# A split value projection, a new order in heads and gates, and a last expert pair by column quarters

## The chip, the cores and the metric

The kernel runs on one core of a Trainium2 chip. Its time is the device time of one execution in microseconds (us). The engines are named as the profile names them: PE is TensorE (PEld its weight loads), DVE is VectorE, ACT is ScalarE, POOL is GpSimd, SP issues most transfers.

## The reference

One layer over 320 tokens (256 prompt frames and 64 sample frames), model width 1024, all in float32:

```python
h   = layer_norm(x)
q, f_pre, i_v, g_o, u_a, u_b, gate_a, gate_b = split(h @ w_in)
logf = log_sigmoid(f_pre) + log1p(lb * exp(-f_pre));  k = (1 - lb) * sigmoid(-f_pre)
# per head (8 heads, 128x128 state): S_t = diag(f_t) S_{t-1} + k_t v_t^T,  o_t = S_t^T q_t
o   = rms_norm(o) * silu(g_o);                 y_a = o @ w_o_a
u   = u_a * sigmoid(u_b);  c = causal depthwise conv, 31 taps;  y_b = silu(layer_norm(c)) @ w_o_b
x   = layer_norm(ALPHA * h + (sigmoid(gate_a) * y_a + sigmoid(gate_b) * y_b) @ w_out)
# router: best of 4 groups, then 2 of its 4 experts
y   = sum_e gates[e] * ((silu(x @ w_gate[e]) * (x @ w_up[e])) @ w_down[e])
out = layer_norm(ALPHA * x + y)
```

## The kernel before

All five engines run programs written out by hand; semaphores alone tie them together, and each engine goes through its program in order. A helper `signal` issues an instruction and then waits for its own end, and a `Chain` does the same.

**Heads.** `head_turn(cur, nxt, prev, pprev)` is one turn of a software pipeline over the eight heads, written once for each engine. In turn n, PE projects the forget logits of head n (`cur_f`) and its queries (`cur_q`); both are split projections (`project`): each float32 operand is a high half in the fp32r format (`wh`, `xh`, written by ACT's `w_high`) and a low half, what is left (`wl`, written by DVE's `w_low`), and PE runs three products for each of 8 row blocks, 24 matmuls of 320 columns. The value projection (`cur_v`, `value_tile`) is not split: 24 matmuls of full float32, tile by tile, whose result has tokens on its rows. For head n-1 PE runs the transposes `prev_kT`, the within-block attention at seven levels of halving (`levels`), `prev_states` and `prev_out`; for head n-2 the sum of squares (`rms`). ACT runs the logarithms and exponentials of the forget gates (`forget`), the copies out of PSUM, `w_high`, and one exponential over all levels (`level_exp`, 2176 columns), then `tile_exp`, `prev_square` and the stores of the states. DVE runs `forget_in` with the scan, `level_decay` (7 instructions), the masks over the level products (`level_mask`, `last_mask`), `w_low`, `prev_final`, `query_side` (7) and `carry_side`. POOL runs `key_decay` (7), seven sums over the levels (`level_sums`, `last_sums`) on which `prev_out` waits, and `key_side` (7).

**Convolution and gates.** PE then runs eight split projections for the convolution (`conv_value`, `conv_gate`) and 24 for the gates (`gates`), with ACT's `u_high`, `t_high` and DVE's `u_low`, `t_low` as their halves. Between these DVE runs the 124 taps of the convolution (`conv_taps`), of which 101 stand ahead of the end of the last `t_low`. PE runs `recurrent(0)` and `(1)` and then sums the columns for the mean, which waits for all taps (`conv_done`).

**Mixing and router.** PE multiplies by `w_out` tile by tile. After the third tile it transposes the new x (`to_features`) and computes the router logits; DVE selects the experts, PE counts positions, and `keep_busy` matmuls, whose result nobody reads, fill PE's time. DVE's `picks` makes the 0/1 matrices by which PE gathers 64 slots for each of two experts.

**Experts.** The 16 experts are taken in 8 pairs. Each pair has 12 groups of weights (4 gate, 4 up, 4 down) of 2 MB each; the ring has 8 slots, and SP reloads a slot when `group_used` says that PE is done with it. `sums_back` puts the sums into PSUM ahead of the last pair's `down`, `last_scatter` adds the last pair's output there, and the closing layer norm (`stats2`, `norm_apply`) reads PSUM and is followed by the store of the result.

Of the kernel before, what the change touches and what calls it, by code (L numbers as in the profile page):

```python
# [21 lines left out]
ALU = mybir.AluOpType  # L22
# [43 lines left out]
def shape_constants():  # L66
# [9 lines left out]
    c[:, COFF["i64"]:COFF["i64"] + CAP] = np.arange(CAP)  # L76
# [10 lines left out]
LOGIT_BANKS = [6, 7, 4]  # L87
# [32 lines left out]
def build(nc, a, o):  # L120
    with ExitStack() as ctx:
# [13 lines left out]
        wring = ring[:, :, :, :, :].rearrange("p g b k n -> p (g b k n)").rearrange("p (g m k n) -> p g m k n", g=SLOTS, m=2, k=2)  # L135
        wslot = ring[:, :, :, :, :].rearrange("p g b k n -> p (g b k n)").rearrange("p (g n) -> p g n", g=SLOTS)
# [50 lines left out]
        (hq, hk, hV, he, hw, hls, hb, heb, hqeb, hkde, hkT, hAM, hAS, hSA, hosq, hrs, hebl, _, hSst, hSo) = carve(  # L187
            0, 2 * T, 2 * T, 384, T, T, T, T, T, T, T, 384, 3 * LW, 384, P, T, T, 4, 892, 2 * P, 2 * P)
# [22 lines left out]
            0, D, 3 * D, KT * NE, NE, *[48] * 8, 72, 24, 24, 144, 18, 20, 4, KT * P, D, D, KT * P, D, 384, 384, 384)  # L211
# [10 lines left out]
        cur = cur.rearrange("p (w t e) -> p w t e", w=3, t=3)  # L222
# [20 lines left out]
                 "osq_ready rms_done rstd_ready rstd_exp o_out so_ready so_stored hc_dve hp_dve hc_act hp_act hc_pool hp_pool v_sb round")  # L243
# [14 lines left out]
                 "eos_ready y_done y_added pick_step gpick_step y_back")  # L258
# [52 lines left out]
        def _(sp):  # L311
# [101 lines left out]
            with sp.Fori(1, PAIRS // 2) as i:  # L413
                for g in range(2 * PARTS):
                    sp.wait_ge(e["group_used"], 2 * PARTS * i + g - SLOTS + 1)
                    load_group(i, g)
            sp.wait_ge(routed, 1)
            more = sp.value_load(flag[0:1, :], min_val=0, max_val=1)
            with sp.If(more != 0):
                with sp.Fori(1, ROUNDS) as r:  # L420
                    with sp.Fori(0, PAIRS // 2) as i:
                        for g in range(2 * PARTS):
                            sp.wait_ge(e["group_used"], PARTS * PAIRS * r + 2 * PARTS * i + g - SLOTS + 1)
                            load_group(i, g)
# [10 lines left out]
        def _(pe):  # L435
# [46 lines left out]
            def cur_f(i, b, first):  # L482
                pe.wait_ge(wlo_ready, 2 * (2 * i + b) + 1)
# [4 lines left out]
            def cur_q(i, b, first, after_rms):  # L488
                pe.wait_ge(wlo_ready, 2 * (2 * i + b) + 2)
# [6 lines left out]
            def value_tile(b, t):  # L496
                t0, n = TILES[t]
                for k in range(KT):
                    last = mm(ps[0:n, 3, t * P:t * P + P], xT[:, k, t0:t0 + n], sh[:, b, 3, k, :], k == 0, k == KT - 1)
                return last  # L500

            def cur_v(i, b, first):
                pe.wait_ge(wh_in[b], i * 48 + (16, 48)[b])
                if not first:
                    pe.wait_ge(h["v_sb"], 2 * i + b)
# [43 lines left out]
            def prev_out(i, b, first):  # L549
# [7 lines left out]
                pe.wait_ge(h["as_ready"], 2 * n1 + 1)  # L557
# [5 lines left out]
                pe.wait_ge(h["as_ready"], 2 * n1 + 2)  # L563
# [9 lines left out]
            def head_turn(cur, prev, pprev, first=False, first_prev=False):  # L573
# [5 lines left out]
                if first or first_prev:  # L579
                    cur_q(*cur, first, False)  # L580
                if pprev:
# [28 lines left out]
            rms(3, 0)  # L610
            prev_kT(3, 1, False)
            levels(3, 1, False)
            prev_states(3, 1)
# [1206 lines left out]
```

## Time and profile before

| what | value |
|---|---|
| time, median of 3 runs | 912.35 us (911.97 to 913.24) |
| the profiled execution | 911.96 us, its span 910.1 us |
| PE busy | 848.2 us, 93% of the span |
| DVE busy | 397.4 us, 44% |
| ACT busy | 227.5 us, 25% |
| POOL busy | 108.1 us, 12% |
| bytes read from HBM | 245.89 MB |

Busy time is what the engine's instructions took; a matmul's end is modelled. Roughly, the heads last from 37 to 178 us, convolution and gates to 314 us, mixing to 412 us, the router to 441 us and the experts to 896 us.

### The profile page before, as it was taken

The numbers are of one execution on the slowest core, as the hardware profiler recorded it, in microseconds if no ns is written. First come the engines' busy times: TensorE is split into PE (matmuls) and PEld (weight loads), VectorE is DVE, ScalarE is ACT, GpSimd is POOL, SyncE is SP. The second block draws the span as 40 slices with busy tenths as digits, with TensorE's granted clock in tenths as the row PEclk, the third lists the DMA queues.
The fourth block names the chain that finished last, engine by engine and source line by source line (L and its number), as shares of the span: only waits on it lengthen the run. The fifth ranks groups of instructions, "written<-read, shape, count | busy, mean of one in ns | idle before, by whom it ended". The sixth has DMA issues, their size and how long they took to land.

```text
span 910.1 us, 12810 instructions
## 1 busy us (share of the span) xinstructions
PE 848.2 (93%) x4904; PEld 532.4 (58%) x4904; DVE 397.4 (44%) x720; ACT 227.5 (25%) x358; POOL 108.1 (12%) x173
## 2 busy tenths in 40 slices
PE   4999999999999999999999999999999899898983
PEld 3989888898989866546554353535435244252330
DVE  6787788879999823215310313103031040310205
ACT  6566666653356131003010011000100001000001
POOL 1366667620000000000000000000000000000000
PEclk9999999999999999998999999999999999999997
DMA  8222222524436523905499999999999999999951
GB/s 302 71 79 80 78 78 85 188 80 154 171 104 237 212 107 153 372 0 208 163 429 428 428 428 428 426 428 427 429 427 429 428 428 428 428 428 428 427 255 59
DMA packets 30420, 248.95 MB, mean 274 GB/s; under 512 B 4462, under 2 KB 7918, under 8 KB 17962
## 3 DMA queue, kind: packets, MB, share of 16 engines
q1 hardware_dynamic: 27840, 247.07, 66.2%
q10 hardware_dynamic: 2538, 1.32, 0.5%
q8 instruction: 27, 0.44, 0.2%
q14 instruction: 15, 0.12, 0.0%
HBM read 245.89 MB, written 2.48 MB: 273 GB/s over the span
## 4 chain that ended last, share of the span: by engine, by line
PE 53%; DVE 19%; DMA 15%; POOL 5%; issue 4%; ACT 3%; POOLq 0%; DVEq 0%; ACTq 0%; SPq 0%
PE ps L437 52%; DMA ring<-in_w_up_e 8%; DMA ring<-in_w_gate_e 7%; DVE ar L1503 6%; DVE split_t L1511 3%; POOL ring L1240 2%; DVE ring L1390 1%; DVE ring L1403 1%; POOL ring L1226 1%; PE ps L772 1%; DVE split_w L1349 1%; POOL ar L1255 0%; DVE mid L1521 0%; POOL ar L1253 0%; DVE split_w L1354 0%
## 5 line engine op out<-in xcount | busy, mean ns | idle before, releaser
L437 PE MATMUL ps<-ring,ar 128*64 128x512 f32 (+1 forms) x1120 | 268.2, 594 | 10.6 <-DMA ring<-in_w_gate_e 3.9
L437 PEld LDWEIGHTS ps<-ring,ar 128*64 128x64 f32 (+1 forms) x1120 | 99.1, 140 | 168.5 <-issue 152.6
L437 PE MATMUL ps<-ring,xT 128*64 128x512 f32 (+2 forms) x896 | 161.4, 458 | 7.0 <-DMA ring<-in_w_gate_e 6.7
L437 PEld LDWEIGHTS ps<-ring,xT 128*64 128x64 f32 (+1 forms) x896 | 84.3, 152 | 79.0 <-issue 63.8
L1720 DVE TENSOR_TENSOR ar<-ar,ps 128x512 f32<-128x512 f32 (+1 forms) x42 | 28.7, 684 | 224.4 <-PE ps L437 224.4
L437 PE MATMUL ps<-split_x,split_t 128*128 128x320 f32 x672 | 101.7, 313 | 4.7 <-DVE split_t L1511 4.1
L437 PEld LDWEIGHTS ps<-split_x,split_t 128*128 128x128 f32 x672 | 100.1, 191 | 6.0 <-issue 3.8
L437 PE MATMUL ps<-split_x,split_w 128*128 128x320 f32 x480 | 80.4, 324 | 6.6 <-DVE split_w L1354 2.7
L437 PEld LDWEIGHTS ps<-split_x,split_w 128*128 128x128 f32 x480 | 73.8, 195 | 11.1 <-issue 2.5
L437 PE MATMUL ps<-ar 128*64 128x64 f32 (+6 forms) x304 | 74.1, 375 | 3.1 <-ACT ar L1174 1.2
L1503 DVE SCALAR_TENSOR_TENSOR ar<-ar,params 128x350 f32<-128x350 f32 x116 | 67.7, 584 | 4.1
L437 PEld LDWEIGHTS ps<-ar 128*128 128x128 f32 (+2 forms) x304 | 35.6, 170 | 39.0 <-DVE ar L1720 19.5
L1708 DVE TENSOR_TENSOR ar<-ar,ps 128x1024 f32<-128x1024 f32 x8 | 9.8, 1222 | 87.5 <-PE ps L437 87.5
L437 PEld LDWEIGHTS ps<-ar,mid 128*128 128x128 f32 x384 | 43.5, 192 | 6.7 <-issue 5.7
L437 PE MATMUL ps<-ar,mid 128*128 128x128 f32 x384 | 45.0, 277 | 0.2 <-DVE ar L1682 0.2
L1240 POOL TENSOR_TENSOR ring<-ring,ar 128x160 f32<-128x160 f32 (+1 forms) x56 | 40.2, 718 | 6.6 <-issue 2.3
L1174 ACT ACTIVATE ar<-ps 128x1024 f32<-128x1024 f32 x8 | 8.2, 1024 | 116.3 <-PE ps L437 116.3
L1164 ACT ACTIVATE ar<-ps 128x1024 f32<-128x1024 f32 x8 | 8.2, 1025 | 111.3 <-PE ps L437 111.3
L1297 DVE BATCH_NORM_STATS2 stats<-ps 128x6 f32<-128x512 f32 (+1 forms) x12 | 8.4, 696 | 61.1 <-PE ps L437 60.8
L437 PE MATMUL ps<-mid,ring 128*128 128x320 f32 x128 | 34.9, 432 | 0.0
L916 ACT ACTIVATE split_t<-ring 128x1024 fp32r<-128x1024 f32 x24 | 25.5, 1061 | 27.3 <-PE ps L437 26.8
L1226 POOL TENSOR_TENSOR ring<-ar 128x160 f32<-128x160 f32 (+1 forms) x56 | 25.7, 459 | 51.8 <-DVE ar L1381 48.0
(190 smaller groups left out, 721.8 us busy)
## 6 DMA issues: line engine op xcount, KB each, us to landing
ring<-in_w_gate_e SPq DMA_DIRECT2D x32, 2048.0 KB, 27.5
ring<-in_w_up_e SPq DMA_DIRECT2D x32, 2048.0 KB, 25.9
ring<-in_w_down_e SPq DMA_DIRECT2D x32, 2048.0 KB, 31.7
ring<-in_w_in SPq DMA_DIRECT2D x56, 512.0 KB, 4.3
ring<-in_w_o_a SPq DMA_DIRECT2D x8, 512.0 KB, 5.9
ring<-in_w_out SPq DMA_DIRECT2D x1, 4096.0 KB, 14.6
ring<-in_w_o_b SPq DMA_DIRECT2D x4, 512.0 KB, 5.1
ar<-in_x_prompt SPq DMA_DIRECT2D x2, 512.0 KB, 4.5
```

The source lines that it names most:

```text
L437: return pe.matmul(out, lhsT, rhs, start=start, stop=stop)
L772: last = pe.transpose(ps[:, k // 4, (k % 4) * P:(k % 4) * P + P], eh[:, k * P:k * P + P], ident)
L916: signal(act, act.activation(t_hi[1 - b][q][1], stl[:, b, 8 * q:8 * q + 8].rearrange("p k n -> p (k n)"), ACT.Copy), thi_ready, 2 * n + q + 1)
L1226: ins = pool.tensor_tensor(xv, bv[:, :, hs - 1:hs].to_broadcast([P, w // (2 * hs), hs]), bv[:, :, 0:hs], ALU.subtract)
L1240: ins = pool.tensor_tensor(xv, xv, kv, ALU.mult)
L1349: signal(dve, dve.tensor_tensor(piece(wl, q), sh[:, b, q].rearrange("p k n -> p (k n)"), piece(whF, q), ALU.subtract), wlo_ready, 2 * n + ...
L1390: ins = dve.tensor_tensor(xv[:, :, hs:2 * hs], bv[:, :, hs:2 * hs], bv[:, :, hs - 1:hs].to_broadcast([P, w // (2 * hs), hs]), ALU.subtract)
L1403: ins = dve.tensor_tensor(xv, xv, qv, ALU.mult)
L1503: vc(dve.scalar_tensor_tensor(acc, uc[:, c, j:j + CW], vt[:, c, j:j + 1], acc, ALU.mult, ALU.add))
L1511: signal(dve, dve.tensor_tensor(t_lo[1 - b][q][1], stl[:, b, 8 * q:8 * q + 8].rearrange("p k n -> p (k n)"), t_hi[1 - b][q][0], ALU.subtract),
L1708: signal(dve, dve.tensor_tensor(eh, ehs, ps[:, 2:4, :].rearrange("p b n -> p (b n)"), ALU.mult), e["eh_ready"], n + 1)
L1720: signal(dve, dve.tensor_tensor(yv, yv, ps[0:c, 4 + j % 2, :], ALU.add), e["y_added"], 6 * n + j + 1)
```

## The change

The value projection becomes a third split projection. Its result has features on its rows, so ACT copies it (`v_features`) and PE transposes it back (`v_tokens`) before the old copy `v_copy`; both copies of V now stand around `level_exp`, `v_features` ahead of it. Each head has one more `w_high` and one more `w_low`. On PE, `levels` goes ahead of `prev_kT`. On DVE, both masks and a new `level_fold` go ahead of `level_decay`; the fold takes over the first of POOL's sums, and POOL's seven sums become three. The copy `hebl` moves from DVE to ACT. `u_high`, `u_low`, `t_high`, `t_low` go by single halves, and fewer taps stand ahead of each `t_low` (98 ahead of the end of the last one). The first tile's transposes go between the second and third tile of the mixing, the second group of logits goes ahead of the third tile's transposes, and the filler matmuls go from 2+8+2 to 6+1. `picks` makes its matrices in one instruction instead of six, as does `gate_picks`; PE starts the gate groups on the first half of the gathered slots. The last pair's `w_down` is stored by column quarters (`w_down_end`, the same bytes) and `down`, copy, scatter and sum go quarter by quarter; `sums_back` is gone.

```diff
 def cur_v(i, b, first):
+    pe.wait_ge(wlo_ready, 3 * n + 3)
+    project(3, piece(wh, 2), piece(wl, 2)).then_inc(h["v_done"], 1)
-    value_tile(b, 0)
-    value_tile(b, 1)
-    value_tile(b, 2).then_inc(h["v_done"], 1)
+def v_tokens(i, b):
+    pe.wait_ge(h["vT_sb"], 2 * i + b + 1)
+    for t, (t0, n) in enumerate(TILES):
+        last = pe.transpose(ps[0:n, 3, t * P:t * P + P], hvT[:, t0:t0 + n], ident)
...
 # PE, head_turn
     if pprev:
         rms(*pprev)
-    if prev:
-        prev_kT(*prev, first_prev)
-        levels(*prev, first_prev)
+        levels(*prev, False)
+        prev_kT(*prev, False)
+        cur_q(*cur, False, True)
         prev_states(*prev)
-    if pprev:
-        cur_q(*cur, False, True)
     cur_v(*cur, first)
     if prev:
         prev_out(*prev, first_prev)
+    v_tokens(*cur)
...
 # PE, router
-keep_busy(2)
 logits(0)
+logits(1)
 to_features(x1, x1_ready, x1T_done, x1T_sb, X1_BANKS, 2, 3)
-logits(1)
 logits(2)
-keep_busy(8)
+keep_busy(6)
...
 # DVE, head_turn
     forget_in(*cur, first or first_prev)
-    level_decay(*cur)
     if prev:
         level_mask(*prev, first_prev)
         last_mask(*prev, first_prev)
+        level_fold(*prev)
+    level_decay(*cur)
...
+def level_fold(i, b):
+    signal(dve, dve.tensor_tensor(hAM[:, :, 0:3 * BLK], hAM[:, :, 0:3 * BLK], hAM[:, :, 4 * BLK:LW], ALU.add), h["fold_ready"], n + 1)
...
 # DVE, picks
-for t in range(3):
-    for m in range(2):
-        ins = dve.tensor_scalar(ePm[:, t, 64 * m:64 * m + 64], i64, cur[:, 0, t, m:m + 1], cur[:, 1, t, m:m + 1], ALU.is_equal, ALU.mult)
+signal(dve, dve.tensor_tensor(pm4, slots_wide, slot_of(cur[:, 0]), ALU.is_equal), e["pick_ready"], n + 1)
...
+def last_down(i, b, c):
+    for k in range(KT):
+        for m in range(2):
+            last = mm(ps[64 * m:64 * m + 64, 6 + c % 2, 0:QN], ehT[:, k, 64 * m:64 * m + 64], w[:, m, k, :], k == 0, k == KT - 1)
...
 # PE, last pair
+last_down(i, b, 0)
+last_down(i, b, 1)
-sums_back()
+last_scatter(0)
+last_down(i, b, 2)
+last_scatter(1)
+last_down(i, b, 3)
+last_scatter(2)
+last_scatter(3)
```

ACT in a turn of the heads, from before the exponential over the levels to the stores of the states. Before, the copy of the queries (L958) and of the crossing blocks (L1005) stand behind the exponential L978, and the copies of V are L970 and L971:

```order
L978 ACTIVATE ring<-ring 128x2176
L958 ACTIVATE ar<-ps 128x320
L1005 ACTIVATE ar<-ps 64x2x64
L986 ACTIVATE ar<-ar 128x320
L988 ACTIVATE ar<-ar 128x128 x2
L988 ACTIVATE ar<-ar 128x64
L895 ACTIVATE split_w<-ring 128x1024
L970 ACTIVATE ar<-ps 128x256
L971 ACTIVATE ar<-ps 64x128
L1021 ACTIVATE ar<-ps 128x320
L1027 DMA out_new_hgrn_prompt<-ar 128x128
```

And now, where the exponential is L1006, `v_features` is L991, the copies of V are L998 and L999, the copy `hebl` is L1015 and the high halves are L919:

```order
L991 ACTIVATE ar<-ps 128x320
L1006 ACTIVATE ring<-ring 128x2176
L998 ACTIVATE ar<-ps 128x256
L999 ACTIVATE ar<-ps 64x128
L1014 ACTIVATE ar<-ar 128x320
L1015 ACTIVATE ar<-ar 128x2
L1017 ACTIVATE ar<-ar 128x128 x2
L1017 ACTIVATE ar<-ar 128x64
L919 ACTIVATE split_w<-ring 128x1024 x2
L1050 ACTIVATE ar<-ps 128x320
L1056 DMA out_new_hgrn_prompt<-ar 128x128
```

The copies of the queries and crossing blocks went ahead of the exponential, a copy of V stands right ahead of it, and between it and the stores stand one more high half and the small copy.

DVE at the start of a turn, from the scan (the last instruction of `forget_in`) on. Before, the seven instructions of `level_decay` are L1390 and the masks L1426 and L1433:

```order
L1381 SCALAR_TENSOR_TENSOR ar<-cst,ar 128x320
L1390 TENSOR_TENSOR ring<-ar 128x2x64
L1390 TENSOR_TENSOR ring<-ar 128x5x32
L1390 TENSOR_TENSOR ring<-ar 128x10x16
L1390 TENSOR_TENSOR ring<-ar 128x20x8
L1390 TENSOR_TENSOR ring<-ar 128x40x4
L1390 TENSOR_TENSOR ring<-ar 128x80x2
L1390 TENSOR_TENSOR ring<-ar 128x160
L1426 TENSOR_TENSOR ar<-ps,mid 128x896
L1433 TENSOR_TENSOR ar<-ps,mid 64x448
```

Now the masks are L1464 and L1471, the fold is L1475 and `level_decay` is L1429:

```order
L1420 SCALAR_TENSOR_TENSOR ar<-cst,ar 128x320
L1464 TENSOR_TENSOR ar<-ps,mid 128x896
L1471 TENSOR_TENSOR ar<-ps,mid 64x448
L1475 TENSOR_TENSOR ar<-ar 128x3x192
L1429 TENSOR_TENSOR ring<-ar 128x2x64
L1429 TENSOR_TENSOR ring<-ar 128x5x32
L1429 TENSOR_TENSOR ring<-ar 128x10x16
```

Masks and fold now stand between the scan and the differences that the exponential over the levels waits for.

PE in the last pair, from the transposes of the gate matrices on. Before, `sums_back` (from `cst`, the identity) stands ahead of `down` (from `ring`):

```order
L776 MATMUL ps<-cst,ar 128x64
L437 MATMUL ps<-ar,cst 128x512 x4
L437 MATMUL ps<-ar,cst 64x512 x2
L437 MATMUL ps<-ring,ar 64x512 x32
L437 MATMUL ps<-ar 128x512 x4
L437 MATMUL ps<-ar 64x512 x2
```

Now two quarters of `down` come first, and scatters of 256 columns stand between the quarters:

```order
L792 MATMUL ps<-cst,ar 128x64
L448 MATMUL ps<-ring,ar 64x256 x32
L448 MATMUL ps<-ar 128x256 x2
L448 MATMUL ps<-ar 64x256
L448 MATMUL ps<-ring,ar 64x256 x16
L448 MATMUL ps<-ar 128x256 x2
L448 MATMUL ps<-ar 64x256
L448 MATMUL ps<-ring,ar 64x256 x16
```

The identity matmuls are gone, and only the scatters of the last two quarters are left behind the last `down`.

## Rows read from the trace of the kernel before

**Rows 1.** Windows: length, busy PE, PEld, DVE, ACT, POOL, PE clock, DMA, GB/s
```profile
460.00:480.00 20.00, 19.52 (x119) 11.51 (x117) 2.60 (x3) 1.63 (x3) 0.00 (x0) 1.00 1.00 428
```

**Rows 2.** Timeline of PE in a turn: start, us, engine, instructions
```profile
85.58 3.78 PE L437 MATMUL ps<-split_x,split_w 128*128 128x320 f32 x24
...
89.20 5.62 PE L437 MATMUL ps<-ring,xT 128*128 128x128 f32 x48
```

**Rows 3.** Timeline of DVE: first instruction of a turn, turns 2 and 7
```profile
62.93 0.49 DVE L1373 SCALAR_TENSOR_TENSOR ar<-ps,ar 128x320 f32<-128x320 f32 x1 [2.55 <-ACT ar L950]
...
163.53 0.49 DVE L1373 SCALAR_TENSOR_TENSOR ar<-ps,ar 128x320 f32<-128x320 f32 x1 [2.26 <-ACT ar L950]
```

**Rows 4.** Timeline of DVE in the heads
```profile
37.87 4.33 DVE L1403 TENSOR_TENSOR ring<-ring,ar 128x128 f32<-128x128 f32 x7
...
85.75 3.39 DVE L1390 TENSOR_TENSOR ring<-ar 128x128 f32<-128x128 f32 x7
...
89.35 1.09 DVE L1426 TENSOR_TENSOR ar<-ps,mid 128x896 f32<-128x896 f32 x1 [0.21 <-DVE ring L1390]
...
90.63 0.62 DVE L1433 TENSOR_TENSOR ar<-ps,mid 64x448 f32<-64x448 f32 x1 [0.19 <-DVE ar L1426]
...
94.40 3.57 DVE L1403 TENSOR_TENSOR ring<-ring,ar 128x128 f32<-128x128 f32 x7
...
98.10 1.38 DVE L1349 TENSOR_TENSOR split_w<-ring,split_w 128x1024 fp32r<-128x1024 f32 x1
```

**Rows 5.** Timeline of ACT in a turn (ACTq: issue of a transfer)
```profile
89.60 2.02 ACT L978 ACTIVATE ring<-ring 128x2176 f32<-128x2176 f32 x1 [2.26 <-POOL ring L1226]
...
96.66 0.38 ACT L970 ACTIVATE ar<-ps 128x256 f32<-128x256 f32 x1 [1.16 <-PE ps L437]
...
98.40 0.39 ACTq L1027 DMA_DIRECT2D out_new_hgrn_sample<-ar  x1
...
100.58 0.44 ACT L944 ACTIVATE ar<-ps 128x320 f32<-128x320 f32 x1 [2.77 <-PE ps L437]
```

**Rows 6.** Timeline of PE in the gates
```profile
224.16 35.46 PE L437 MATMUL ps<-split_x,split_t 128*128 128x320 f32 x240 [1.66 <-DVE split_t L1511]
...
261.79 37.06 PE L437 MATMUL ps<-split_x,split_t 128*128 128x320 f32 x240 [2.17 <-DVE split_t L1511]
```

**Rows 7.** A window of PE: length, busy, PE clock, DMA, GB/s
```profile
263.00:264.00 1.00, 1.00 (x5) 0.50 0.00 0
```

**Rows 8.** Timeline where taps end and the mean begins
```profile
313.95 0.58 DVE L1505 SCALAR_TENSOR_TENSOR mid<-ar,params 128x350 f32<-128x350 f32 x1
...
314.91 2.52 PE L437 MATMUL ps<-mid,ones 128*128 128x350 f32 x8
```

**Rows 9.** Timeline of the router, from the last logits to the first gate group
```profile
418.06 4.11 PE L437 MATMUL ps<-ar,xT 128*128 128x16 f32 x32
...
429.87 0.07 DVE L1656 MEMSET ar<- 64x16 f32 x1
...
431.16 0.32 PE L437 MATMUL ps<-ar,cst 128*128 128x48 f32 x2
...
432.46 2.07 DVE L1682 TENSOR_SCALAR ar<-cst,ar 128x64 f32<-128x64 f32 x6
...
434.58 5.62 PE L437 MATMUL ps<-ar,mid 128*128 128x128 f32 x48 [0.20 <-DVE ar L1682]
...
441.10 11.38 PE L437 MATMUL ps<-ring,ar 128*64 128x512 f32 x52 [0.90 <-ACT ar L1160]
```

**Rows 10.** Timeline of the last pair and the closing norm
```profile
869.34 5.53 PE L437 MATMUL ps<-ar,cst 128*128 128x512 f32 x12 [1.03 <-ACT ar L1170]
...
874.80 13.95 PE L437 MATMUL ps<-ring,ar 128*64 128x512 f32 x64
...
889.94 5.57 PE L437 MATMUL ps<-ar 128*128 128x512 f32 x12 [1.18 <-ACT ar L1174]
...
898.82 1.28 DVE L1301 SCALAR_TENSOR_TENSOR ar<-ps,mv,mid 128x1024 f32<-128x1024 f32 x1 [1.55 <-issue]
```

More of the change, by code:

```diff
@@ L416, in _ @@
                     load_group(i, g)
+            end_i = PAIRS // 2 - 1
+            for g in range(2 * PARTS):
+                sp.wait_ge(e["group_used"], 2 * PARTS * end_i + g - SLOTS + 1)
+                if g < 2 * PARTS - 4:
+                    load_group(end_i, g)
+                else:
+                    sp.dma_start(wslot[:, g % SLOTS, :], column(a["w_down_end"], g % 4)).then_inc(group_in[g % SLOTS], 16)
             sp.wait_ge(routed, 1)
@@ L784, in down, with scatter @@
                     both(6, ehT, g).then_inc(e["group_used"], 1)
-            def scatter(n):
-                pe.wait_ge(e["eos_ready"], n + 1)
+            def scatter(n, late=0):
+                pe.wait_ge(e["eos_ready"], n + 1 + 3 * late)
                 pe.wait_ge(e["eGT_sb"], n + 1)
@@ L846, in late_pair @@
                 down(n, i, b)
-                scatter(n)
+                scatter(n, 1)
             more = pe.value_load(flag[0:1, :], min_val=0, max_val=1)
@@ new lines, in gates @@
+                signal(act, act.activation((mT, sgb)[q][:, bass.ds(n - 4, 1), :].rearrange("p o n -> p (o n)"), ps[:, GATE_BANKS[2 * b + q], 0:T], ACT.Sigmoid), sgt_ready, 2 * n + q + 1)
+            for i in range(2):
+                for b in range(2):
+                    for q in range(2):
+                        t_high(i + 1, b, q)
+                        out_gates(i, b, q)
+            with act.Fori(2, NG // 2 - 1) as i:
+                for b in range(2):
+                    for q in range(2):
+                        t_high(i + 1, b, q)
+                        gates(i, b, q)
@@ L1129, in _ @@
+            for b in range(2):
+                for q in range(2):
+                    gates(NG // 2 - 1, b, q)
             act.preload_act_table_set("natural_log_exp_and_others")
@@ L1181, in expert_pair @@
                 hidden_copy(n)
-                down_copy(n)
+                if end:
+                    for c in range(4):
+                        last_copy(c)
+                else:
+                    down_copy(n)
             def late_pair(i, b):
@@ L1196, in _ @@
             expert_pair(PAIRS // 2 - 1, 1, end=True)
+            act.preload_act_table_set("natural_log_exp_and_others")
+            for t in range(3):
+                rstd_of(var2, rstd2, step, t)
             more = act.value_load(flag[0:1, :], min_val=0, max_val=1)
             with act.If(more != 0):
+                act.preload_act_table_set("silu_and_others")
                 with act.Fori(1, ROUNDS) as r:
@@ L1462, in head_turn @@
                     w_low(*nxt, 0)
+                else:
+                    u_low(0, 0)
                 if prev:
@@ L1467, in head_turn @@
                 query_side(*cur)
+                carry_side(*cur, first)
                 if nxt is None:
-                    u_low(0)
+                    u_low(0, 1)
                 elif not first:
                     w_low(*nxt, 1)
-                carry_side(*cur, first)
+                if nxt:
+                    w_low(*nxt, 2)
             head_turn((0, 0), (0, 1), None, None, first=True)
@@ L1482, in _ @@
             last_mask(3, 1, False)
+            level_fold(3, 1)
             pprev_out(3, 0)
-            u_low(1)
+            u_low(1, 0)
+            u_low(1, 1)
             vc = Chain(dve, conv_step)
```

435 lines of the change are left out of this document (221 added, 214 removed).

## The prediction

> **What bounds the kernel now.** I read the page first (PE busy 93%, every other engine under half), then the chain of waits, then windows of 20 us, and last the timeline of each stage, since the change touches all of them but the middle of the experts.
>
> The experts are bound by the transfers, although PE looks full: in [rows 1] the DMA engines are busy all of the time at 428 GB/s, and each group of weights is awaited. The stream begins when the first slot comes free and its bytes are fixed. So the expert stage moves as a block with its start, and what shortens PE's work inside it (halves of the gathered slots, fewer matrix instructions) is worth nothing there. Only its start and what lies behind the last transfers can give time.
>
> In the heads a turn lasts 20.12 us (five turns between the two starts of [rows 3]). PE is nearly full in it, but it isn't alone: VectorE starts each turn after waiting 2 us or so for ScalarE's logarithms [rows 3]. VectorE's own work in a turn is thus about 18.1 us. From the convolution on, PE and VectorE are level: the last tap ends 0.4 us before the mean that needs it [rows 8], and PE waits 1.66 and 2.17 us for low halves [rows 6].
>
> **Heads.** A value projection takes 5.62 us now and a split one 3.78 us [rows 2]; with some 0.6 us of transposes back, PE saves 1.2 us a turn. I don't count it, because two other loops become longer.
>
> ScalarE with VectorE: from the end of the exponential over the levels, 91.62, to the end of the second store's issue, 98.79, is 7.17 us [rows 5]. Of it 1.16 us were a wait for V and 1.04 us the two copies that go ahead; a second high half adds 1.09 (those are 128x1024 like the first), the small copy 0.23 and the wait to begin 0.17: 6.46 us. `forget` takes 2.8 us (100.58 to VectorE's start of the turn at 103.4). VectorE's `forget_in` and scan take 2.7 us (83.05 to 85.75 in the turn of [rows 4]). Then come the masks, 1.09 + 0.19 + 0.62 us [rows 4], and the fold of 576 columns, by the 1.38 us of 1024 columns [rows 4] about 0.8; with their gaps 2.9 us. `level_decay` takes 3.4 us and the exponential 2.02, with gaps 5.6. The loop is 6.46 + 2.8 + 2.7 + 2.9 + 5.6 = 20.46 us. Before, the masks ran under the exponential and cost this loop nothing.
>
> VectorE alone: 18.1 + 0.8 (fold) + 0.1 + 1.5 (a third low half) - 0.4 (copy gone) = 20.1 us if its queries take 3.57 us, and 20.9 us if they take the 4.33 us of the turn in which POOL's keys ran beside all of them [rows 4]. I take 20.45 us a turn, +0.33, five times: +1.6 us. The first two turns: VectorE goes from its queries to the next turn in one piece, so the third low half less the copy costs 1.2 us; in the second turn the masks come into the loop, +0.9. So the last turn begins 3.7 us later, at 167.2 instead of 163.53.
>
> The two prices of the queries differ by what POOL did beside them: 3.57 us where its keys ran beside only the second half, 4.33 us where they ran beside all of them [rows 4]. In the new order queries and keys both begin when the exponential ends, or nearly. The Trainium skill, "GPSIMD Engine Reference" (Key points), says that GpSimd shares its SBUF interfaces with VectorE and that instructions of VectorE with two SBUF inputs contend with it; by that rule the sum below would be 3.2 us larger (rival B), by the shorter row as it stands. The trace agrees in these two rows.
>
> **Convolution and gates.** In the last turn PE waits some 3 us for `prev_square`, which now stands behind three high halves; a wait of 2.17 us made the PE clock fall to half for about 3 us [rows 6, 7], so I put 1.0 us on the levels behind it. Against that, `u_low(2)` no longer stands behind eight taps, 0.5 us. Fewer taps ahead of each `t_low` take away PE's waits of 1.66 and 2.17 us, but VectorE has the same 124 taps and halves to do and is without a pause, so `conv_done` is where VectorE puts it; PE, 4 us early, then waits in front of the mean in one piece, is ready a little sooner (-0.2), and restarts at half clock: by the two equal stretches of 240 matmuls in [rows 6], 37.06 - 35.46 = 1.6 us. From there to the router PE is the bound, so all of this counts: 1.0 - 0.5 - 0.2 + 1.6 = +1.9 us.
>
> **Router.** The last logits end 1.1 us earlier: two groups of logits, 4.1 us with the third [rows 9], no longer stand behind the third tile's transposes, but one tile's transposes (1.0 us) came ahead of the third tile's mix. The selection ended at 429.94 and PE came to it at 431.16, late by its own filler [rows 9]; with six fillers it comes on time: 428.9. PE's counts and one filler then take 2.3 us, VectorE's picks 0.6 instead of 2.07 (384 columns at the rate of the fold), so the gather begins at 431.2 instead of 434.58. The first gate group began 0.9 us after the gather's end, after a copy [rows 9]; it now starts on the first half at once: 436.9 instead of 441.1. -4.2 us.
>
> **Last pair.** 869.34 to 874.87 are `sums_back` [rows 10], which goes. The four quarters of `down` cost as many columns, 13.95 us, and two scatters of a quarter (5.57 / 4 = 1.4 us each) lie between them: 869.3 + 13.95 + 2.8 = 886.1. Two more scatters: 888.9, where PE's last matmul ended at 895.5 before. PE took its four groups without a wait, the last from 885.3 on [rows 10]; the last quarter now begins at 882.6, and if its weights landed only at 885.3, 2.7 us of this would be lost. VectorE then has for each tile an add of 256 columns (0.45), statistics of 512 (0.7) and a short one (0.3) behind the last scatters: to 892.5. The branch, 1.55 us [rows 10], now stands behind the norm. Six instructions of 1.3 us end at 900.4 instead of 906.7. -6.3 us; the copies of a quarter, 0.3 to 0.4 us on ScalarE, lie beside matmuls, and if they didn't it would be 1 us more.
>
> **Sum.** 3.7 + 1.9 - 4.2 - 6.3 = -4.9 us. The profiled execution took 911.96 us, so 907.0; the median of the runs is 0.4 above it: **907.4 us**, 0.5% faster. 0.2% (1.8 us) is about what a measurement of this kernel can tell from no change.
>
> **Rivals.**
>
> A. PE was the bound of the heads and the reordered loops fit around it: a turn becomes 20.12 - 1.2 = 18.9 us. For it: the page's 93%. Against: VectorE's 20.1 us. Seven turns give -8.4 instead of +3.7, so 895.3; halfway, with a turn of 19.5 us, five of them give -3.1 and the sum 902.7. Chance 0.2 together.
>
> B. VectorE and POOL disturb each other fully: the turn is 20.9 us, and the masks wait now and then. +0.45 for six turns, and 0.5 for the second turn: 910.6. Chance 0.15.
>
> C. The PE clock falls in every turn. PE now waits between the next forget projection and `rms`, because ScalarE's square comes late: its projection ends some 14.7 us into the turn and the square 16.6, 1.9 us. The trace has 1.66 us without and 2.17 us with a fall [rows 6, 7]. If it falls, levels, queries and V lie in the slow stretch, each turn loses 1.6 us less 0.15 us of slack, six times 8.7 us, and 0.7 in the second: 916.8, slower. It decides from 1.3 us a turn. Chance 0.07. In a sentence of its own: the Trainium skill, "TensorE: Matmul & The Clock Gate" (HAM oscillation), warns of exactly this, a clock that falls again at each repeated idle stretch.
>
> D. The router's filler is now too short and the gather runs at half clock. Half speed for 3 us of the gather gives 2.8 back at most: 910.2. Chance 0.08.
>
> E. The last pair's narrower matmuls don't run in pairs at full rate: 256 columns behind each weight load instead of 512. A fifth more on 13.95 us is 2.8 us: 910.2. Chance 0.05.
>
> The forecast itself: 0.45, within 904 to 909.5.
>
> **Numbers.** The range is 898 to 912: below it lies half of A, above it C and the ends of B and D. Faster by over 0.2% means below 910.5: forecast, A, and parts of B, D and E: 0.78. Within: 0.13. Slower: 0.09.
>
> **What would show it.** Turn starts of VectorE 20.3 to 20.6 us apart, and the last at about 167; at 163 or below, A. No long wait of VectorE for ScalarE's logarithms ahead of a turn. PE's idle time per turn in one or two pieces near 2 us with the clock at 1.00 (C: 0.5 in windows). A wait of PE ahead of the mean, which begins near 318.9, and none over 1 us in the gates. The first gate group at about 442.5. PE's last scatter 6.6 us nearer to the last landing than before, the norm's end 6.3. The prediction is wrong if a turn is off by half a microsecond (3 us in all), or if the transfers have slack that I don't see, so that the start of the stream doesn't set their end.

## The result, and the profile after

The changed kernel takes **921.88 us** (median, 921.66 to 925.07) beside 912.80 us for the kernel before on the same chip: ratio 1.0108, 95% interval 1.0085 to 1.0132. It is slower by 1%, where 907.4 us were forecast and 898 to 912 us allowed. The profiled execution has a span of 919.6 us where before had 910.1: +9.5 us.

I split these 9.5 us at the places at which the prediction split its sum. First the heads: VectorE's first instruction of turns 2 and 7 (start, us, instruction, in brackets the wait and its releaser), to be held against [rows 3].

```profile
66.58 0.49 DVE L1412 SCALAR_TENSOR_TENSOR ar<-ps,ar 128x320 f32<-128x320 f32 x1 [1.55 <-ACT ar L973]
...
179.95 0.49 DVE L1412 SCALAR_TENSOR_TENSOR ar<-ps,ar 128x320 f32<-128x320 f32 x1 [1.97 <-ACT ar L973]
```

The last turn starts at 179.95 instead of 163.53: **+16.4 us** (forecast +3.7). Five turns take 22.67 us each, not 20.12. Then the mean, on PE's timeline, for [rows 8]:

```profile
317.18 8.78 PE L448 MATMUL ps<-mid,ring 128*128 128x320 f32 x32
332.13 5.04 PE L448 MATMUL ps<-mid,ones 128*128 128x350 f32 x8 [6.18 <-DVE mid L1554]
```

It starts 17.2 us later than before (314.91), 0.8 us more than the heads explain, after a wait of 6.18 us for the last tap, and takes 5.04 us instead of 2.52 since the clock has fallen: **+3.3 us** (forecast +1.9). The first gate group, the first quarters of `down` and the last instruction of the norm answer to [rows 9, 10]:

```profile
451.32 5.62 PE L448 MATMUL ps<-ar,mid 128*128 128x128 f32 x48
456.88 13.52 PE L448 MATMUL ps<-ring,ar 128*64 128x512 f32 x62
...
884.40 7.13 PE L448 MATMUL ps<-ring,ar 128*64 128x256 f32 x64 [0.48 <-ACT ar L1203]
...
914.93 1.28 DVE L1341 SCALAR_TENSOR_TENSOR ring<-ring,rstd,ar 64x1024 f32<-64x1024 f32 x1
```

The gate group starts 15.8 us later than at 441.10, so the router gave 16.4 + 3.3 - 15.8 = **4.0 us** (forecast 4.2). The norm ended at 906.69 and now ends at 916.21, +9.5, so the last pair gave 15.8 - 9.5 = **6.3 us** (forecast 6.3). Three of the four terms are right within 1.4 us; the heads are off by 12.7.

Where the heads lose them is seen in the turn that starts at 90.19. ScalarE from the copy `v_features` (L991) on:

```profile
99.30 0.44 ACT L991 ACTIVATE ar<-ps 128x320 f32<-128x320 f32 x1 [3.45 <-PE ps L448]
99.90 2.02 ACT L1006 ACTIVATE ring<-ring 128x2176 f32<-128x2176 f32 x1 [0.17 <-DVE ring L1429]
103.58 0.38 ACT L998 ACTIVATE ar<-ps 128x256 f32<-128x256 f32 x1 [1.66 <-PE ps L517]
```

The exponential ends at 101.92, but on ScalarE all that stands behind it, up to the next turn's `forget`, waits for `v_copy` (L998), and `v_copy` waits 1.66 us for the transposes `v_tokens` (L517). PE at that time, and VectorE from the masks on:

```profile
100.97 1.69 PE L448 MATMUL ps<-ar 128*128 128x128 f32 x10 [1.77 <-DVE mid L1493]
102.59 0.90 PE L517 MATMUL ps<-cst,ar 128*128 128x128 f32 x3
```

```profile
92.90 1.09 DVE L1464 TENSOR_TENSOR ar<-ps,mid 128x896 f32<-128x896 f32 x1 [0.21 <-DVE ar L1420]
94.18 0.62 DVE L1471 TENSOR_TENSOR ar<-ps,mid 64x448 f32<-64x448 f32 x1 [0.19 <-DVE ar L1464]
94.83 0.76 DVE L1475 TENSOR_TENSOR ar<-ar 128x576 f32<-128x576 f32 x1
95.63 4.19 DVE L1429 TENSOR_TENSOR ring<-ar 128x128 f32<-128x128 f32 x7
99.98 0.55 DVE L1493 SCALAR_TENSOR_TENSOR mid<-ps,params,ar 128x320 f32 x1 [0.16 <-DVE ring L1429]
```

The transposes stand behind `prev_out`, and `prev_out` waits 1.77 us for `pprev_out` (L1493), which frees its bank and stands behind masks, fold and `level_decay` on VectorE. In the kernel before it stood behind `level_decay` and the masks too, and nobody waited for it:

```profile
109.50 5.62 PE L437 MATMUL ps<-ring,xT 128*128 128x128 f32 x48
111.83 0.55 DVE L1451 SCALAR_TENSOR_TENSOR mid<-ps,params,ar 128x320 f32 x1 [0.17 <-DVE ar L1433]
115.06 1.10 PE L437 MATMUL ps<-ar 128*128 128x128 f32 x8
```

In this turn, which starts at 103.40, it ended 9.0 us into the turn, and PE came to `prev_out` only at 11.7, after its long value projection. In the changed kernel it ends 10.3 us into the turn, because of the fold and the slower `level_decay`, and PE, with the shorter projection, is there already at 9.0. So PE's wait is new, but `prev_out` itself comes no later in the turn than before; what is new is that ScalarE's copy stands behind it and ahead of `tile_exp`. And `level_decay` (L1429) takes 4.19 us instead of 3.39 [rows 4]. Over the heads, the waits by engine, line and releaser (total, times, longest) are:

```profile
PE ps L448 <- ACT ar L1050: 11.6, 7, 3.1
PE ps L448 <- DVE mid L1493: 10.3, 6, 2.0
...
ACT ar L991 <- PE ps L448: 24.0, 7, 3.5
ACT ar L998 <- PE ps L517: 8.0, 6, 2.2
```

L1050 is `prev_square`, for which `rms` waits. The largest number, 24.0 us ahead of `v_features`, is not the one that counts: in five of the turns the exponential behind it still waits for `level_decay`, above for 0.17 us.

**Theory.** The heads lose 8 us to `v_copy` ahead of `tile_exp`, which hands every lateness of PE to the next turn, and 4 us to the slower `level_decay` (0.7 us a turn by the rows, over six turns). **Rivals:** the falls of PE's clock; PE's loop through `prev_square`; the masks ahead of `level_decay` by themselves; the split itself.

### The profile page after: what moved, and what is told of

It is laid out like the page before. It is cut to its first block, busy times and chain, and to the rows that moved or that the text cites. A ratio compares the mean times of both kernels' runs of the same rounds, so it can differ in the third digit from the quotient of the medians.

```text
span 919.6 us, 12462 instructions
## 1 busy us (share of the span) xinstructions
PE 837.2 (91%) x4790; PEld 529.4 (58%) x4790; DVE 399.1 (43%) x661; ACT 241.8 (26%) x385; POOL 80.2 (9%) x141
## 3 DMA queue, kind: packets, MB, share of 16 engines
q10 hardware_dynamic: 2538, 1.32, 0.5%
## 4 chain that ended last, share of the span: by engine, by line
PE 52%; DVE 21%; DMA 16%; ACT 8%; issue 2%; ACTq 1%; DVEq 0%; SPq 0%
PE ps L448 50%; DMA ring<-in_w_gate_e 11%; DVE ar L1552 7%; DMA ring<-in_w_up_e 4%; DVE ring L1429 3%; DVE split_t L1559 3%; ACT split_w L919 2%; ACT ar L1017 1%; DVE ar L1464 1%; DVE ar L1475 1%; DVE ar L1420 1%; DMA ar<-in_x_prompt 1%; ACTq L1056 1%; PE ps L788 1%; ACT ar L973 1%
## 5 line engine op out<-in xcount | busy, mean ns | idle before, releaser
L448 PE MATMUL ps<-ring,ar 128*64 128x512 f32 (+2 forms) x1184 | 269.6, 571 | 10.4 <-DMA ring<-in_w_gate_e 3.9
L448 PEld LDWEIGHTS ps<-ring,ar 128*64 128x64 f32 (+1 forms) x1184 | 103.7, 140 | 163.2 <-issue 146.1
L448 PE MATMUL ps<-split_x,split_w 128*128 128x320 f32 x672 | 115.9, 331 | 8.4 <-ACT ar L1062 3.3
L448 PE MATMUL ps<-ring,xT 128*64 128x512 f32 x512 | 116.2, 594 | 6.9 <-DMA ring<-in_w_gate_e 6.9
L448 PEld LDWEIGHTS ps<-split_x,split_w 128*128 128x128 f32 x672 | 107.7, 203 | 14.0 <-ACT ar L1062 2.9
L448 PEld LDWEIGHTS ps<-ring,xT 128*64 128x64 f32 x512 | 41.6, 136 | 77.1 <-issue 67.8
L448 PE MATMUL ps<-ar 128*64 128x64 f32 (+8 forms) x316 | 75.3, 370 | 10.8 <-DVE mid L1493 10.3
L1272 POOL TENSOR_TENSOR ring<-ar 128x160 f32<-128x160 f32 (+1 forms) x56 | 28.3, 505 | 80.4 <-DVE ar L1420 76.6
L1286 POOL TENSOR_TENSOR ring<-ring,ar 128x160 f32<-128x160 f32 (+1 forms) x56 | 30.4, 544 | 26.0 <-ACT ring L1006 16.5
L1429 DVE TENSOR_TENSOR ring<-ar 128x160 f32<-128x160 f32 (+1 forms) x56 | 30.5, 544 | 1.9
```

The source lines that it names most:

```text
L448: return pe.matmul(out, lhsT, rhs, start=start, stop=stop)
L1272: ins = pool.tensor_tensor(xv, bv[:, :, hs - 1:hs].to_broadcast([P, w // (2 * hs), hs]), bv[:, :, 0:hs], ALU.subtract)
L1286: ins = pool.tensor_tensor(xv, xv, kv, ALU.mult)
L1429: ins = dve.tensor_tensor(xv[:, :, hs:2 * hs], bv[:, :, hs:2 * hs], bv[:, :, hs - 1:hs].to_broadcast([P, w // (2 * hs), hs]), ALU.subtract)
```

## The experiments

All times are medians, with the ratio to the kernel before and its 95% interval; "turn" is the mean of the five turns 2 to 7. The first three, `copy_late` and `filled` are made on the changed kernel, `copy_sync` and `copy_decay` on copy_late.

### out_first: `pprev_out` ahead of the masks

```diff
 # DVE, head_turn
+    pprev_out(*pprev)
     level_mask(*prev, first_prev)
     last_mask(*prev, first_prev)
     level_fold(*prev)
     level_decay(*cur)
-    pprev_out(*pprev)
```

> Edit: on VectorE the output of the head before the last (pprev_out, 0.55 us) goes ahead of masks, fold and decay. The theory: a turn of the heads is 22.7 us instead of 20.1 because ScalarE's v_copy, which stands ahead of all that follows the exponential, waits 1.0 to 2.2 us (8.0 us in 6) for v_tokens, and these stand on PE behind prev_out, which waits for pprev_out (10.3 us in 6). Two loops run through this wait: one by VectorE (masks, fold, decay, exponential, copies, forget) and one by PE (rms, levels, queries, V, v_features, exponential, copies, high halves, prev_square, rms). If the PE loop sets the turn, the whole wait is given back: 6 turns by 1.3 us, about 914 us. If the VectorE loop does, pprev_out itself (0.59 us) now lies in it: about 918 us. The rivals (VectorE slowed by POOL, or PE's slow clock) expect no change, 921 to 923 us.

918.32 us (1.0056, 1.0039 to 1.0073), turn 21.71 us. `v_copy` waits no more, and the time is that of the second case: the loop by VectorE, with `pprev_out` in it, sets the turn. PE's waits for `prev_square` grew from 11.6 to 18.9 us while the turn became shorter.

### square_first: `prev_square` ahead of two high halves

```diff
 # ACT, head_turn
     tile_exp(*cur, first)
+    prev_square(*prev, first_prev)
     w_high(*nxt, 1)
     w_high(*nxt, 2)
-    prev_square(*prev, first_prev)
     store_states(*prev)
```

> Edit: on ScalarE prev_square goes ahead of the two high halves (2.2 us), the stores stay behind them. The PE loop (PE waits 11.6 us in 7 for prev_square before rms) becomes 2.2 us shorter, the VectorE loop stays as it is. If the PE loop alone sets the turn, about 911 us; if the VectorE loop is as long, no change (within 1 us of 922) and PE's wait only moves from rms to another place.

918.31 us (1.0051, 1.0035 to 1.0067), turn 22.48 us. Between the two cases: PE's waits for `prev_square` fell from 11.6 to 1.0 us, but 13.5 us in 6 for `rstd` came ahead of the queries, and ScalarE's copy of the queries, ahead of the exponential, waits 8.8 us instead of 2.6. The waits for `v_copy` fell to 1.9 us in 2, and yet the turn is only 0.2 us shorter: the wait mostly moved.

### decay_first: `level_decay` ahead of the masks

```diff
 # DVE, head_turn
+    level_decay(*cur)
     level_mask(*prev, first_prev)
     last_mask(*prev, first_prev)
     level_fold(*prev)
-    level_decay(*cur)
```

> Edit: on VectorE level_decay goes back ahead of masks and fold, as before the change. The VectorE loop becomes 2.6 us shorter, the PE loop stays. If the VectorE loop alone sets the turn, about 909 us; if the PE loop does or both are level, no change to speak of (within 2 us of 922): the exponential then waits for v_features, which wait for PE's V projection (24.0 us in 7).

935.32 us (1.0250, 1.0233 to 1.0268), turn 24.28 us. I expected no case of this kind. The waits say why:

```profile
PE ps L448 <- POOL ar L1300: 21.4, 7, 3.4
...
ACT ar L998 <- PE ps L517: 20.1, 6, 4.1
```

With the masks late POOL's sums (L1300) are late, `prev_out` waits for them, and `v_copy` for the transposes behind it, 20.1 us instead of 8.0. It is the theory's mechanism, made worse, and the turn became 1.6 us longer. And the loop by VectorE did not become 2.6 us shorter, as I had expected. ScalarE in the turn that starts at 118.58:

```profile
126.07 0.27 ACT L1034 ACTIVATE ar<-ps 64x128 f32<-64x128 f32 x1 [3.53 <-DVE ar L1464]
...
128.24 2.02 ACT L1006 ACTIVATE ring<-ring 128x2176 f32<-128x2176 f32 x1
```

L1034 is the copy of the crossing blocks. It waits for the mask L1464, and the change put it ahead of the exponential. So the exponential begins 9.7 us into the turn here and 9.7 us in the changed kernel (99.90 in the turn from 90.19), whichever of masks and `level_decay` comes first; in the kernel before, with this copy behind it, it began at 6.6 us (89.60 from 83.05). This run therefore doesn't say what the masks in VectorE's loop cost.

### tail_router: heads, convolution and gates as before

The edit takes back all parts of the change up to the gates; those of the router and the last pair stay.

> Edit: heads, convolution and gates as before; only the router part (first tile's transposes, logits, fillers, picks, gate groups on the first half) and the last pair by column quarters are new. By the stages of the two traces router and last pair together gave 10 to 11 us: 902 us. If the gain of either hangs on the late start of the stream, or the transfers have slack, it would be less: 905 to 908 us.

**902.37 us** (0.9885, 0.9868 to 0.9901). The two late parts give 10.4 us, with 10.5 forecast. The rest of the change costs 19.5 us.

### copy_late: `v_copy` in its old place

```diff
 # ACT, head_turn
-    v_copy(*cur, first)
     tile_exp(*cur, first)
     w_high(*nxt, 1)
     w_high(*nxt, 2)
+    v_copy(*cur, first)
     prev_square(*prev, first_prev)
```

> Edit: the changed kernel with ScalarE's v_copy back behind tile_exp and the high halves, its place before the change; all else of the change stays. The theory (v_copy ahead of tile_exp hands PE's lateness on to forget): the wait of 8.0 us in 6 goes as with out_first, and pprev_out does not enter the VectorE loop, so a turn of 21.1 us: about 915 us. If v_copy's place costs nothing by itself (the masks ahead of decay are all of it): 918 to 922 us.

**913.61 us** (1.0010, 1.0000 to 1.0020), turn 21.15 us. One line moved gives 8.3 us, and PE waits as long for `pprev_out` as in the changed kernel; only ScalarE's `tile_exp` and high halves no longer stand behind that wait. VectorE, turns 2 and 7, and the waits:

```profile
65.92 0.49 DVE L1412 SCALAR_TENSOR_TENSOR ar<-ps,ar 128x320 f32<-128x320 f32 x1 [1.61 <-ACT ar L973]
...
171.66 0.49 DVE L1412 SCALAR_TENSOR_TENSOR ar<-ps,ar 128x320 f32<-128x320 f32 x1 [0.99 <-ACT ar L973]
```

```profile
PE ps L448 <- DVE mid L1493: 10.2, 6, 2.0
PE ps L448 <- ACT ar L1050: 7.0, 4, 2.4
```

### split_old: the split value projection in the old order

On tail_router. PE, ScalarE and VectorE keep the order of before; `v_features` stands behind `tile_exp`, `v_copy` where it was, the fold behind the masks.

> Edit: tail_router (heads in the order of before) with the split value projection: third high and low half, v_features behind tile_exp, v_copy in its old place, v_tokens, the fold on VectorE behind the masks and POOL's three sums. The theory (the orders cost, not the split): PE is the bound of the heads before and has 1.2 us less to do, but prev_out now waits for POOL's sums; 899 to 903 us. If the split itself is what costs (halves on ScalarE and VectorE, contention): over 906 us.

920.43 us (1.0092, 1.0073 to 1.0111), turn 21.92 us: far off, 18 us slower than tail_router. PE has less to do and waits 18.4 us in 7 for POOL's sums ahead of `prev_out`, with the transposes and the next forget projection behind it. The last turn starts 16.4 us later than in tail_router. Of this 9.0 us lie in the five turns, and 5.0 us are there when the second head's turn starts (48.77 instead of 43.76), by this edit's own place for `v_features`: in the first turn it stands behind `tile_exp`, PE waits 6.42 us for it, and the two projections behind that wait take 9.75 us instead of tail_router's 7.31, at a granted clock of 0.50 to 0.72 from 38 to 46 us. So the new order is not the only culprit: in this form of the old one the split gains nothing either, since what PE saves is spent in front of the sums. The change's order with `v_copy` late (copy_late) is the better home for it.

### gates_new, gates_rec, tail_rec: the wait in front of the mean

gates_new is tail_router with the new gates (`t_high`, `t_low` by halves, new places of the taps). gates_rec adds this, and tail_rec is this on tail_router without the new gates:

```diff
 # PE, after the gates
     recurrent(1)
+    recurrent(2)
     pe.wait_ge(conv_done, 4)
...
     last.then_inc(cmean_done, 1)
-    recurrent(2)
     recurrent(3)
+    recurrent(4)
```

> Edit: tail_router with the gates by single halves (t_high, t_low) and the new places of the taps; heads and the halves for the convolution as before. The theory: PE loses its waits of 1.66 and 2.17 us in the gates and gets one in front of the mean, in one piece, and restarts at half clock. In the changed kernel the mean began 0.8 us later against the heads, and 2.5 us went at half clock: 905.5 us, 3 us slower than tail_router. If the order of the taps costs nothing: 902.4 us.

904.11 us (0.9905, 0.9888 to 0.9921): 1.7 us slower than tail_router, not 3. Its mean began 0.8 us earlier than tail_router's and took 4.94 us instead of 2.52.

> Edit: gates_new with PE's recurrent(2) ahead of the mean, so that 4.4 us of its wait are filled with work, and recurrent(4) ahead of the variance in its place. If the wait ahead of the mean and the slow clock behind it are the price of the new gates, both go (4.4 + 2.5 us): 899 to 900 us. If VectorE's taps set the time whatever PE does meanwhile, 905 us as gates_new.

**897.70 us** (0.9835, 0.9819 to 0.9851), the fastest of all. In PE's timeline the wait is 1.88 us and the mean runs at full clock:

```profile
301.35 13.08 PE L448 MATMUL ps<-mid,ring 128*128 128x320 f32 x48
316.32 2.62 PE L448 MATMUL ps<-mid,ones 128*128 128x350 f32 x8 [1.88 <-DVE mid L1542]
```

> Edit: tail_router (gates as before) with recurrent(2) ahead of the mean. There PE is not early, the mean follows recurrent(1) without a wait. If PE's own work sets the time there, the order is worth nothing: 902.4 us. Then the new gates alone cost 1.7 us, recurrent(2) alone gives nothing, and both together gave 4.7 us (gates_rec).

902.92 us (0.9898, 0.9881 to 0.9914), as tail_router. So the new gates alone cost 1.7 us, `recurrent(2)` alone gives nothing, and the two together give 4.7: the gates gather PE's waits into one, and only then is there something to fill. The 1.7 us are small (the intervals of the two ratios overlap); that they are real I take from the trace, where 0.8 us earlier and 2.4 us slower give 1.6.

### copy_sync: both decays begin together

```diff
 # POOL, head_turn, on copy_late
+    pool.wait_ge(h["fold_ready"], 2 * cur[0] + cur[1])
     key_decay(*cur)
```

> Edit: copy_late, with POOL's key_decay waiting for VectorE's fold, so that both decays begin together, as in the kernel before. There VectorE's level_decay took 3.39 us beside POOL's 3.70; in the changed kernel it starts 2.8 us behind POOL's and takes 3.98 to 4.20. If that offset costs the 0.8 us, level_decay is back at 3.4 us; POOL ends some 0.3 us behind it, so 0.4 us a turn is won: about 911 us. The sums come 2.5 us later, though, and prev_out, v_tokens and the next forget projection stand behind them: by that loop a turn of 20.8 us at least, and if it is longer than that the time stays at 913 to 915 us. If the 0.8 us have another cause, level_decay stays at 4.0 to 4.2 us.

927.81 us (1.0169, 1.0151 to 1.0188), turn 23.42 us. The two questions have two answers. `level_decay` is back at its old time:

```profile
120.52 3.39 DVE L1431 TENSOR_TENSOR ring<-ar 128x128 f32<-128x128 f32 x7
```

But the late sums cost more than that: PE waits 24.7 us in 7 for them.

### copy_decay: copy_late with `level_decay` ahead of the masks

> Edit: copy_late with level_decay ahead of masks and fold. If the masks ahead of level_decay are what the heads still lose (2.6 us a turn in VectorE's loop and 0.8 us of slower decay), the time falls to 903 to 906 us. The theory: with the masks late another loop binds, VectorE's masks and fold, POOL's sums, prev_out, v_tokens, the next forget projection, as in split_old (turns of 20.8 to 21.9 us, PE waiting 18.4 us in 7 for the sums): 912 to 919 us.

920.98 us (1.0088, 1.0067 to 1.0110), turn 22.07 us. As the theory had it, a little beyond its range: PE waits 21.0 us in 7 for the sums. With ScalarE's new order the masks ahead of `level_decay` are no fault; behind it they cost more. As in decay_first the exponential stays where it was, 9.6 to 9.7 us into the turn, held by the copy of the crossing blocks; no run moved masks and this copy back together in the new order.

### after_mended: the changed kernel with two lines mended

The edits of copy_late and gates_rec, on the changed kernel.

> Edit: the changed kernel with v_copy in its old place (copy_late) and recurrent(2) ahead of the mean. If the two losses are independent, 913.6 - 6.4 = 907.2 us; what is left against gates_rec (897.7 us), 9.5 us, is then the heads: VectorE's loop with the masks in it.

907.32 us (0.9946, 0.9930 to 0.9963): the losses add up. It is 9.6 us above gates_rec, which differs from it above all by the heads: the last turn starts at 171.82 instead of 163.39.

### filled: four matmuls over the wait ahead of `rms`

```diff
 # PE, head_turn, on the changed kernel
...
+    for _ in range(4):
+        mm(ps[:, 4, 0:T], ident, xT[:, 0, :], True, True)
     rms(*pprev)
```

> Edit: the changed kernel with four matmuls (320 columns, identity by xT, some 1.4 us, into a bank that the levels overwrite) ahead of rms in each turn, where PE waits for prev_square (11.6 us in 7). Rival C of the prediction (the falls of PE's clock cost time in the heads): the granted clock in the heads' windows, now 0.91 to 1.00, goes to 1.00 and the time falls by 1 to 5 us, 917 to 921. If the slow stretches lie beside waits anyway: 922 us as the changed kernel.

920.24 us (1.0075, 1.0055 to 1.0096). The same windows of PE (length, busy, clock, DMA, GB/s), here and then in the changed kernel:

```profile
100.00:120.00 20.00, 20.00 (x172) 0.91 0.27 88
120.00:140.00 20.00, 17.49 (x163) 1.00 0.26 88
140.00:160.00 20.00, 17.66 (x166) 1.00 0.25 88
```

```profile
100.00:120.00 20.00, 17.07 (x156) 0.91 0.26 88
120.00:140.00 20.00, 16.64 (x154) 0.91 0.26 88
140.00:160.00 20.00, 15.72 (x157) 1.00 0.26 88
```

The clock is up, not everywhere: of the nine such windows from 20 to 200 us seven are at 1.00 here, and two in the changed kernel. `v_copy` waits 6.1 instead of 8.0 us. By the medians that gives 1.6 us, and by the ratios 3.0. By the turns it is 2.0: the last one starts 2.7 us earlier (177.26 instead of 179.95), but 0.7 of that is there already at the start of turn 2 (65.91 instead of 66.58), before any of the added matmuls can act on it. The two ratios' intervals overlap. I call the price of these falls 2 to 3 us, an estimate, and no main cause.

### f_first, f_first2, f_first3: what bounded the heads before

All on gates_rec, with the value projection not split.

```diff
 # PE, head_turn: f_first
-    cur_f(*cur, first)
...
     cur_v(*cur, first)
+    cur_f(*nxt, False)
     prev_out(*prev, first_prev)
 # PE: rms behind the levels
 # ACT: prev_square behind the next forget
 # f_first2: v_copy behind the next forget too
 # f_first3: on PE levels, rms, prev_kT, cur_q, prev_states
```

> Edit: gates_rec (heads as before the change, V not split) with PE's next forget projection ahead of prev_out, rms behind the levels, and ScalarE's prev_square behind the next forget. The reading to be tested: a turn of 20.12 us before the change was a loop by VectorE's masks, POOL's sums (ended 13.07 us into the turn), prev_out, forget projection (3.6) and ScalarE's logarithms. With the projection ahead of prev_out the sums are out of it, and a turn is bound by PE's own 19.1 us: five turns and a half by 1.0 us less, 892 us. If PE's own work or VectorE was already the bound at 20.1 us: 897.7 us as gates_rec.

907.54 us (0.9942, 0.9929 to 0.9954), 10 us slower than gates_rec: I had overlooked that `v_copy` waits for `prev_out`, 27.5 us in 6.

> Edit: f_first with ScalarE's v_copy behind the next forget as well. In f_first v_copy waits 27.5 us in 6 for prev_out (both use the buffer of V), which now stands behind the forget projection, and forget stands behind v_copy: the change's own fault once more, a copy ahead of the logarithms that waits for prev_out. With it out of the way the projection ends 15.4 us into the turn and VectorE's next turn can start 18.3 us after the last; PE's own work is 19.1 us, VectorE's 18.1: five and a half turns by 1.0 us less than 20.12, 892 us. If the heads were bound by PE or VectorE at 20.1 us in truth: 897 to 898 us, as gates_rec.

899.30 us (0.9852, 0.9838 to 0.9865). Turns of 20.14 to 20.31 us from the third on: taking POOL's sums out of the loop won nothing. PE waits 7.8 us in 6 for VectorE's `carry_side` behind `prev_out` instead.

> Edit: f_first2 with PE's levels ahead of the key transposes, as in the changed kernel, so that PE does not wait for VectorE's carry_side (7.8 us in 6) right behind prev_out. In f_first2 a turn is still 20.25 us: 18.8 us of PE's work and 1.3 us of this wait. If PE's own work was the bound of the heads, and what stood on top of it handed-over waits of 1 us or so, a turn is now 18.9 to 19.3 us: 891 to 893 us. If VectorE's 18.1 us with its own hand-overs binds at 20.1, the time stays at 898 to 899 us.

898.24 us (0.9842, 0.9828 to 0.9856). VectorE's turn starts:

```profile
60.30 0.49 DVE L1417 SCALAR_TENSOR_TENSOR ar<-ps,ar 128x320 f32<-128x320 f32 x1 [0.24 <-DVE ar L1461]
84.19 0.49 DVE L1417 SCALAR_TENSOR_TENSOR ar<-ps,ar 128x320 f32<-128x320 f32 x1 [0.53 <-ACT ar L977]
104.49 0.49 DVE L1417 SCALAR_TENSOR_TENSOR ar<-ps,ar 128x320 f32<-128x320 f32 x1 [0.58 <-ACT ar L977]
124.23 0.49 DVE L1417 SCALAR_TENSOR_TENSOR ar<-ps,ar 128x320 f32<-128x320 f32 x1 [0.53 <-ACT ar L977]
143.94 0.49 DVE L1417 SCALAR_TENSOR_TENSOR ar<-ps,ar 128x320 f32<-128x320 f32 x1 [0.43 <-ACT ar L977]
163.68 0.49 DVE L1417 SCALAR_TENSOR_TENSOR ar<-ps,ar 128x320 f32<-128x320 f32 x1 [0.51 <-ACT ar L977]
```

The last three turns take 19.7 us, below the 20.12 of before, with the same work on VectorE. So VectorE's 18.1 us with its own hand-overs did not bind at 20.12. That PE's work with some exposed hand-overs did is argued, not shown: from 140 to 160 us PE is busy in 19.45 of the 20 us here and in 19.51 in the kernel before. The turn from 60.30 takes 23.9 us and eats the gain; PE waits 3.2 us for POOL's keys once and ScalarE 8.3 us in 4 for weights from memory. Neither of the two makes it so long: f_first2 has as long a turn there (23.8 us) with 0.4 us of waits for the keys, and ScalarE's rows of that turn show no wait for weights. In both runs ScalarE waits 5.4 to 5.5 us in it for `rms`, which these edits put behind the levels on PE; no run takes that wait away.

## Why the prediction was wrong, point by point

- **What bounds the heads: wrong.** I read VectorE's wait for the logarithms [rows 3] as the sign that VectorE and ScalarE set the turn. The row that says otherwise stood in [rows 5]: ScalarE itself waited 2.77 us for PE's forget projection ahead of `forget`. PE was nearer to being the bound: f_first3 shows that VectorE's work alone did not hold the turn at 20.12 us, and the step to PE is argued from its busy time. Yet rival A was no case: what the split saves on PE is spent in front of POOL's sums in the old order (split_old), and in front of `pprev_out` and `prev_square` in the new one.
- **Heads, the failed step: "Of it 1.16 us were a wait for V ... 6.46 us".** I took V's wait out of ScalarE's stretch, since V comes earlier. But `v_copy` no longer waits for the projection; it waits for `v_tokens`, these for `prev_out`, and this for `pprev_out`, which fold and decay now end later while PE comes earlier. The wait that I put at nothing measured 8.0 us in 6, up to 2.2. I priced every instruction that was moved and did not ask what the copy waits for in its new place, ahead of `tile_exp`. 8.3 us (copy_late) of the 12.7.
- **Heads, the second term: mis-sized.** "`level_decay` takes 3.4 us": it took 3.98 to 4.20 in the seven turns with masks, 4.1 us over turns 1 to 6, as read from the trace; in copy_sync, where both decays begin together, it took 3.39 us again. With it VectorE's loop of 20.46 us becomes 21.2, and copy_late's turn is 21.15. That makes 4.2 of the remaining 4.4 us, by the sum: no run shows it as a gain in time, since copy_sync lost more at the sums.
- **Rival B** had the right kind of cause, at the wrong instruction and by too little. The queries took 3.9 to 4.2 us.
- **Rival C** came true as a sight (clock below 1.00 in seven of the nine windows from 20 to 200 us) and hardly as a price (filled).
- **Convolution and gates, +1.9 for +3.3.** The fall behind the mean's wait was right, at 2.5 us instead of 1.6; the mean was 0.5 us later than reckoned, although the levels at half clock (+1.0) did not happen, so 1.5 us of it stay without a cause. The new gates by themselves brought the mean 0.8 us earlier (gates_new), so they lie between the last turn's start and the gates.
- **Router -4.2 for -4.0, last pair -6.3 for -6.3, rivals D and E: right.** tail_router shows both without the rest.
- **The range** ended at 912 because the only slower cases were one loop longer by a known row. None held a wait of `v_copy` that the new order creates.

## What to carry to other kernels

For every instruction that a change moves, ask what it waits for in its new place and who waits for its result, and then what stands behind that waiter in its engine's order, until the chain comes back; a copy ahead of work that the next turn needs makes the whole turn as late as its slowest source. An edit that takes a step out of a loop tests that loop only if nothing else holds the same place: in decay_first the exponential began no earlier. When an engine waits in front of the supposed bound, look one engine further: [rows 5] named PE. A wait that has been gathered into one piece is worth nothing until independent work of its size is put there (1.7 us lost without, 4.7 us won with).

## What the runs showed of the hardware

- **The same seven instructions of VectorE take 3.39 or up to 4.20 us by how they stand to POOL's.** `level_decay` took 3.39 to 3.43 us beside POOL's `key_decay` when both began together (the kernel before, decay_first, copy_decay, copy_sync), and 3.98 to 4.20 when it began 2.8 us behind, while POOL's, 3.6 to 3.7 us there, took 4.00 to 4.20. The Trainium skill, "GPSIMD Engine Reference" (Key points), says that VectorE's instructions with two SBUF inputs contend with GpSimd. The slower rows agree; no run has `level_decay` without POOL beside it, so whether the 3.39 us hold such a price too stays open. POOL's sum L1299 showed the like, in most turns 0.46 us in copy_late and 1.32 in copy_decay and copy_sync.
- **PE's clock did not follow the length of the last wait.** Windows of 1 us of the changed kernel (length, busy, clock, DMA, GB/s): after a wait of 1.38 us (up to 168.65) the clock falls to half while PE is busy, and in and after one of 3.13 us (up to 198.87) it stays at full.

```profile
168.00:169.00 1.00, 0.35 (x3) 1.00 0.00 0
...
171.00:172.00 1.00, 1.00 (x6) 0.50 0.40 90
...
196.00:197.00 1.00, 0.00 (x0) 1.00 0.14 57
197.00:198.00 1.00, 0.00 (x0) 1.00 0.00 0
...
200.00:201.00 1.00, 1.00 (x41) 1.00 0.23 66
```
